# Attention in two blocks: heads paired by query block, weight rounding on ScalarE, and the sink as a column

## What is computed

```python
# block one, each of two layers
o_a = mla_attention(...)       # all 512 keys; q.k over 96 features, v of 64
o_c = windowed_gqa(...)        # keys of the blocks b-1, b, b+1; ALiBi bias; 64 features
m = max(max(s), sink); e = exp(s - m)
probs = e / (sum(e) + exp(sink - m))
# block two
yc = dsa_attention(...)        # causal, keys of the blocks 0..b, mask of the top 128; 64 features
```

## Time and profile before

| | |
|---|---|
| median of 3 runs | 2979.09 us (2977.27 to 2981.9) |
| the profiled execution, its own time | 2981.74 us |
| its span in the profile | 2979.9 us |
| TensorE busy | 2826.6 us, 95% |
| VectorE, ScalarE, GpSimd busy | 1519.9, 1077.5, 446.4 us |
| mean granted TensorE clock | 0.975 |

### The profile page before, as it was taken

How to read it: one execution, slowest core, us unless ns; L and a number is a source line. 1 busy time by engine, 2 the same in 40 slices (tenths; PEclk the granted TensorE clock), 3 DMA queues, 4 the chain that set the end, 5 groups by cost and what they waited for, 6 DMA issues and landing times. The chain is left out here.

```text
span 2979.9 us, 36682 instructions
## 1 busy us (share of the span) xinstructions
PE 2826.6 (95%) x13172; PEld 2236.6 (75%) x13172; DVE 1519.9 (51%) x2343; ACT 1077.5 (36%) x1713; POOL 446.4 (15%) x319
## 2 busy tenths in 40 slices
PE   5999999999999899999999999989998899899998
PEld 4874678888887687467888888767686588688886
DVE  5556673533324656667353333455588635643423
ACT  4345333422224534533342222443623324532221
POOL 1010111311102201011121110220101112211101
PEclk9999999999999899999999999999997899999999
DMA  3320012222222232001222222212231122122232
GB/s 130 125 88 29 29 58 86 84 99 96 101 100 99 75 118 85 29 29 57 96 75 99 98 100 99 99 59 83 77 121 57 43 85 71 57 85 94 90 112 85
DMA packets 37056, 245.92 MB, mean 83 GB/s; under 512 B 4144, under 2 KB 5168, under 8 KB 7984
## 3 DMA queue, kind: packets, MB, share of 16 engines
q1 hardware_dynamic: 33600, 239.09, 22.8%
q10 hardware_dynamic: 3312, 4.93, 0.5%
HBM read 241.91 MB, written 2.10 MB: 82 GB/s over the span
## 5 line engine op out<-in xcount | busy, mean ns | idle before, releaser
L529 PE MATMUL bank<-h_hi,w_hi 128*128 128x512 f32 (+1 forms) x2280 | 884.7, 388 | 22.6 <-DVE w_lo L1466 10.6
L531 PE MATMUL bank<-h_hi,w_lo 128*128 128x512 f32 (+1 forms) x2280 | 866.0, 380 | 0.0
L530 PE MATMUL bank<-h_lo,w_hi 128*128 128x512 f32 (+1 forms) x2280 | 865.8, 380 | 0.0
L1466 DVE TENSOR_TENSOR w_lo<-raw,w_hi 128x2048 fp32r<-128x2048 f32 x223 | 515.2, 2311 | 532.1 <-ACT w_hi L1011 373.6
L529 PEld LDWEIGHTS bank<-h_hi,w_hi 128*128 128x128 f32 x2280 | 432.2, 190 | 118.5 <-issue 30.6
L531 PEld LDWEIGHTS bank<-h_hi,w_lo 128*128 128x128 f32 x2280 | 432.1, 189 | 81.1
L530 PEld LDWEIGHTS bank<-h_lo,w_hi 128*128 128x128 f32 x2280 | 432.4, 190 | 79.2 <-issue 3.6
L1011 ACT ACTIVATE w_hi<-raw 128x2048 fp32r<-128x2048 f32 x141 | 269.3, 1910 | 225.0 <-PE bank L531 218.4
L529 PE MATMUL bank<-a_hi,w_hi 128*128 128x512 f32 x528 | 205.7, 390 | 0.0
L531 PE MATMUL bank<-a_hi,w_lo 128*128 128x512 f32 x528 | 205.7, 390 | 0.0
L530 PE MATMUL bank<-a_lo,w_hi 128*128 128x512 f32 x528 | 205.7, 390 | 0.0
(11 more groups left out here) (383 smaller groups left out, 4166.9 us busy)
## 6 DMA issues: line engine op xcount, KB each, us to landing
raw<-in_stream SPq DMA_DIRECT2D x226, 1024.0 KB, 4.9
x<-in_xT SPq DMA_DIRECT2D x2, 1024.0 KB, 12.6
out_T<-x ACTq DMA_DIRECT2D x8, 256.0 KB, 2.1
p_f<-in_pT ACTq DMA_DIRECT2D x2, 512.0 KB, 3.9
memf<-in_memT ACTq DMA_DIRECT2D x1, 1024.0 KB, 5.5
cst_sb<-in_cst ACTq DMA_DIRECT2D x1, 411.5 KB, 6.6
pos_i<-in_pos ACTq DMA_DIRECT2D x1, 258.0 KB, 9.2
vec<-in_vec ACTq DMA_DIRECT2D x2, 26.0 KB, 1.7
```

The source lines that it names most:

```text
L529: nc.tensor.matmul(ps, wh, xh, start=start, stop=False)
L530: nc.tensor.matmul(ps, wh, xl, start=False, stop=False)
L531: return nc.tensor.matmul(ps, wl, xh, start=False, stop=stop)
L1466: nc.vector.tensor_tensor(w_lo[s][:, :], raw[s][:, :], w_hi[s][:, :].bitcast(F32), ALU.subtract).then_inc(lo_ready, 1)
```

## The change

Three parts. **Order:** in `mla`, `gqa` and `dsa` the items go two heads at a time by query block: (0,b0), (1,b0), (0,b1), (1,b1) and so on (`items_of`). The value products move from once a head to once a query block of the pair (`values_of_pair`), and alternate between the two halves of the output. In the biased attentions both scores of a pair are issued together, at even steps, behind a wait until VectorE is through with the maximum of all items before (`shift_ready`). The output tile is taken at the next pair's first block. **Rounding:** ScalarE rounds the woven-in units (`split_unit` in ScalarE's `after_blocks`); GpSimd's `split_units` is gone. **Sink:** column 0 of each `gqa` probability tile holds sink/scale, which ScalarE writes; the maximum and the exponential run over it too. Two VectorE instructions an item go (L1661 or L1662, and L1671), and on ScalarE a one-column copy takes the place of the one-column exponential. The diff, cut:

```diff
-    stage("z1b", A=1, HP=1), stage("mla", I=32, H=8, O=4), stage("gqa", I=32, H=8, O=4),
-    stage("am", A=8, HP=1), stage("cm", A=8, R=8),
+    stage("z1b", A=1), stage("mla", I=32, H=16, O=4), stage("gqa", I=32, H=16, O=4),
+    stage("am", A=8), stage("cm", A=8, R=8),
...
+        def items_of(a):
+
+            if a["per_tile"] == 2:
+                return [(2 * pair + one, b) for pair in range(a["heads"] // 2) for b in range(ST) for one in range(2)]
+            return [(h, b) for h in range(a["heads"]) for b in range(ST)]
...
             def attention(c, st, ready, also=None):
                 a = ATT[st]
-                items = [(h, b) for h in range(a["heads"]) for b in range(ST)]
+                items = items_of(a)
                 for sem_, value in ready:
                     pe.wait_ge(sem_, value)
+                def scores(t):
+                    h, b = items[t]
+                    ks = a["keys"](b)
+                    nc.tensor.matmul(SCORES[t % 2][:, 0:len(ks) * P], a["q"](h, b), a["k"](h, ks),
+                                     start=True, stop=True).then_inc(logits_done, 1)
                 for t in range(len(items) + LAG):
-                    if t < len(items):
-                        h, b = items[t]
+                    if t < len(items) and a["biased"]:
+                        if t % 2 == 0:
+                            if t >= 2:
+                                pe.wait_ge(shift_ready, c.at("I", st, t))
+                            scores(t)
+                            scores(t + 1)
+                    elif t < len(items):
                         if t >= 2:
                             pe.wait_ge(exp_done, c.at("I", st, t - 1))
-                        ks = a["keys"](b)
-                        nc.tensor.matmul(SCORES[t % 2][:, 0:len(ks) * P], a["q"](h, b), a["k"](h, ks),
-                                         start=True, stop=True).then_inc(logits_done, 1)
+                        scores(t)
...
                             mm = nc.tensor.transpose(TURNED[:, j * P:(j + 1) * P],
-                                                     a["prob"][i % 4][:, j * P:(j + 1) * P], ident)
+                                                     a["prob"][i % 4][:, lo + j * P:lo + (j + 1) * P], ident)
                         mm.then_inc(turned, 1)
-                        if b == ST - 1 and h >= 1:
+                        if a["per_tile"] == 2:
+                            if i >= 2 and i % 2 == 0:
+                                values_of_pair(c, st, i // 2 - 1)
+                        elif b == ST - 1 and h >= 1:
                             values(c, st, h - 1)
                     if also is not None:
                         also(t)
-                values(c, st, a["heads"] - 1)
+                if a["per_tile"] == 2:
+                    values_of_pair(c, st, len(items) // 2 - 1)
+                else:
+                    values(c, st, a["heads"] - 1)
...
+            def values_of_pair(c, st, q):
+
+                a = ATT[st]
+                pair, b = q // ST, q % ST
+                pe.wait_ge(turn_taken, c.at("I", st, 2 * q + 2))
+                if b == 0 and (pair >= 1 or st != "mla"):
+                    pe.wait_ge(o_split, c.at("O", st, pair))
+                ks, at = a["keys"](b), slice(b * P, b * P + P)
+                for j, t in enumerate(ks):
+                    for one in range(2):
+                        mm = nc.tensor.matmul(VALUES[64 * one:64 * one + 64, at], a["v"](2 * pair + one, t), a["pT"][one][:, j, at],
+                                              start=j == 0, stop=j == len(ks) - 1)
+                mm.then_inc(head_done, 1)
...
-                items = [(h, b) for h in range(a["heads"]) for b in range(ST)]
+                items = items_of(a)
+
+                def set_sink(t):
+                    nc.scalar.activation(a["prob"][t % 4][:, 0:1], vv("sink", items[t][0]), ACT.Copy,
+                                         scale=1 / a["scale"]).then_inc(sink_set, 1)
+                for t in range(4) if sink else ():
+                    set_sink(t)
...
-                        if sink:
-                            nc.scalar.activation(st_snk[:, t:t + 1], vv("sink", h), ACT.Exp, bias=st_neg[:, t:t + 1])
+                        n += a.get("first", 0)
                         src = a["prob"][t % 4] if a["biased"] else SCORES[t % 2]
                         nc.scalar.activation(a["prob"][t % 4][:, 0:n], src[:, 0:n], ACT.Exp, bias=st_neg[:, t:t + 1],
                                              scale=a["scale"], accum_out=st_sum[:, t:t + 1]).then_inc(exp_done, 1)
+                        if sink and t + 4 < len(items):
+                            act.wait_ge(exp_done, c.at("I", st, t + 1))
+                            set_sink(t + 4)
                     if t >= LAG:
                         h, b = items[t - LAG]
-                        if b == ST - 1 and h >= 1 and h % a["per_tile"] == 0:
-                            output_hi(c, st, h // a["per_tile"] - 1)
+                        if a["per_tile"] == 2 and b == 0 and h % 2 == 0 and h >= 2:
+                            output_hi(c, st, h // 2 - 1)
+                        elif a["per_tile"] == 1 and b == ST - 1 and h >= 1:
+                            output_hi(c, st, h - 1)
...
+                    if b % BLK == BLK - 1 or b == TILES[st][-1][-1]:
+                        split_unit(c, st, b // BLK)
...
+                if t in (23, 31):
+                    split_unit(c, "mv", (t - 23) // 8)
...
-                            link(nc.vector.scalar_tensor_tensor(out=src[:, 0:n], in0=tile, scalar=factor, in1=SCORES[t % 2][:, 0:n],
+                            lo = a.get("first", 0)
+                            link(nc.vector.scalar_tensor_tensor(out=src[:, lo:lo + n], in0=tile, scalar=factor, in1=SCORES[t % 2][:, 0:n],
                                                                 op0=ALU.mult, op1=ALU.add))
+                            n += lo
+                        if sink:
+                            dve.wait_ge(sink_set, c.layer * len(items) + (t + 1))
                         link(nc.vector.reduce_max(st_max[:, t:t + 1], src[:, 0:n], AX_X))
-                        if sink:
-
-                            link(nc.vector.tensor_scalar(st_neg[:, t:t + 1], st_max[:, t:t + 1], a["scale"], vv("sink", h), ALU.mult, ALU.max))
-                            nc.vector.tensor_scalar(st_neg[:, t:t + 1], st_neg[:, t:t + 1], -1.0, None, ALU.mult).then_inc(shift_ready, 1)
-                        else:
-                            nc.vector.tensor_scalar(st_neg[:, t:t + 1], st_max[:, t:t + 1], -a["scale"], None, ALU.mult).then_inc(shift_ready, 1)
+                        nc.vector.tensor_scalar(st_neg[:, t:t + 1], st_max[:, t:t + 1], -a["scale"], None, ALU.mult).then_inc(shift_ready, 1)
+                    if a["per_tile"] == 2 and t % 8 == 3 and 11 <= t < len(items):
+                        output_lo(c, st, taken)
+                        taken += 1
                     if 1 <= t <= len(items):
...
-                        if sink:
-                            link(nc.vector.tensor_tensor(st_sum[:, i:i + 1], st_sum[:, i:i + 1], st_snk[:, i:i + 1], ALU.add))
                         link(nc.vector.reciprocal(st_rec[:, i:i + 1], st_sum[:, i:i + 1]))
-                        p = a["prob"][i % 4]
+                        p = a["prob"][i % 4][:, a.get("first", 0):]
                         nc.vector.tensor_scalar(p[:, 0:n], p[:, 0:n], st_rec[:, i:i + 1], None, ALU.mult).then_inc(prob_ready, 1)
...
-            def split_units(c, st):
-
-                for u, (kind, n) in enumerate(releases(st)):
-                    v = c.base[st]["U"] + u + 2
-                    pool.wait_ge(tile_done if kind == "T" else part_done, c.at(kind, st, n))
-                    pool.wait_ge(raw_ready[v % 2], c.raw(v))
-                    nc.gpsimd.tensor_tensor(w_hi[v % 2][:, :], raw[v % 2][:, :], ones[:, 0:1].to_broadcast([P, UC]), ALU.mult).then_inc(pool_hi_ready, 1)
```

64 lines of the change are left out of this document (19 added, 45 removed).

## The result

| | before | changed |
|---|---|---|
| median | 2980.49 us (2977.27 to 2982.55, 4 runs) | 2896.3 us (2893.83 to 2896.46, 4 runs) |
| span of the profiled execution | 2979.9 us | 2894.6 us |
| mean granted clock | 0.975 | 0.982 |

The account below looks back on a forecast made before the run. TensorE was taken as the bound; 2 x 15.2 (`gqa`) + 2 x (8.3 - 1.9) (`mla`) + 15 (`dsa`) = 58.2 us off 2981.7 gives 2923.5, by the runs' median 2921, stated as 2920; range 2893 to 2950 at 80%.

Parts of the forecast that it names:

- The frame: Whole kernel: TensorE is busy for 2826.6 of 2979.9 us, so its own work or its waits are what count.
- the forecast itself: Whole kernel: the main case, 2920 us, with its own range of 2900 to 2945 and a chance of 70%.
- rival 5: More than forecast: `dsa` returns to full clock early and no pair waits, 85 us gained, 2894 or a little less; 7%.
- Scores in pairs: In `gqa` and `dsa`, the second score of a pair is free: 11.7 us saved per `gqa`, 11.7 in `dsa` at full clock.
- Value products: Neighbours on different output halves overlap fully: 6.7 us saved per `gqa`, 8.3 per `mla`, 6.7 in `dsa` at full clock.
- Rival 1: Value products don't overlap at 128 columns: 55 us of the gain go, 2975, at best 2965; 8%.
- my ground for the overlap: At the end of `mla` before the change, 8 value records start within 1.30 us, so each half keeps its rate.
- `gqa`'s waits: In each `gqa`, TensorE waits for VectorE at the pairs of steps 12 and 28: 2 x 1.6 = 3.2 us lost.
- The rounding in `mla`: In each `mla`, a rounding on ScalarE falls where a step of TensorE is short: 1.9 us added on the path.
- 27 + 7 - 19: In `dsa`: 27 us of saved work at its mean clock, 7 of waits gone, 19 taken back: net 15, between 0 and 32.
- I take back 6 + 13 = 19: In `dsa`, waits for VectorE: four `w_lo` of some 1.5 us each, and 0.8 us at the other pairs.
- The signs: Changed profile: `gqa` at full clock, idle at most 10 us; scalings never 3 us; roundings 1.9 us, no wait for the copy.

Follow-up runs that it names:

- experiment 1: The kernel before with only the rounding of the woven-in weights moved from GpSimd to ScalarE, old order kept: 2967.8 us median, ratio 0.9972.
- experiment 2: The changed kernel with the rounding of the woven-in weights back on GpSimd: 2900.2 us median.
- experiment 1 to 5: Step from experiment 1 to the changed kernel with each `gqa` and `dsa` score issued at its own step again: 2923.2 us median.
- experiment 3: The changed kernel with the sink as before, a one-column exponential on ScalarE and two more VectorE instructions per `gqa` item: 2906.2 us median.

## Why the prediction was right or wrong

**The frame held.** TensorE's own time was what counted: its work at full clock fell by 73.9 us where I had 71.8. The time lies in the range, at its low end, but it is outside the 2900 to 2945 that I gave to the forecast itself with 70%. The likeliest was 24 us too high, and the range holds the result because it was stretched to take in most of rival 5, to which I gave 7%. Rival 5 had the size right and half of the reason: the clock of `dsa` came back, but it also said that no pair waits, and in `dsa` ten did.

**Scores in pairs: right.** Four records last as long as two (0.85 us), 11.7 us a `gqa`.

**Value products: right in mechanism, the size a little low in `mla`.** A group of `mla` takes 1.02 to 1.03 us and a step of 0.10 into it (four transposes take 0.53 before a group, 251.51 to 252.04, and 0.43 before a score); I had 1.19 with the step. What I missed is that the old groups paid that step too. By the trace an `mla` has 10.4 us less work, forecast 8.3. In `gqa` 8 groups at 0.59, 8 at 0.81 and a step of some 0.12 into each make 13.1 us (forecast 13.8). Rival 1 falls: its group would have lasted 2.1 us. One count in my ground for the overlap was off: the earlier trace rows counts records in flight, and 7, not 8, start within the 1.30 us; that each half keeps its rate stands.

**`gqa`'s waits: right.** 2.9 us at two places, forecast 3.2 at two. What I left out is that half of the woven-in blocks now lead into transposes, 0.08 us cheaper each: 1.3. 11.7 + 7.4 + 1.3 - 2.9 = 17.5, measured 17.1.

**The rounding in `mla`: wrong sign.** I had 1.9 us more of waits. In the old order it would have been nearly so: a wait of 1.7 us for the copy, and with the clock that fell behind it 3.0 (experiment 1). In the new one that wait is 0.7 us (the row at 260.23), since a value group of 1.02 us stands ahead of it, and the stage is 0.7 faster than with GpSimd's rounding (experiment 2). Idle time fell by 1.1 us in all: 3.0 to the good of the forecast. 6.4 + 2.1 (work) + 3.0 (waits) = 11.5, as measured.

**`dsa`: the two terms that failed.** The range was right; what was mis-sized is the sum of this paragraph, 27 + 7 - 19. Its 27 keeps the stage's clock at its old mean: 18.4 of work and 8.6 of clock. Its "I take back 6 + 13 = 19" are the waits, and the 13 counts 0.8 for all 16 pairs where the sentence leaves four out (12 would be 9.6). Measured from first to last score, 101.8 us became 76.7: 15.8 of work, 17.7 of half-clock loss as the mean clock rose from 0.75 to 0.90, and 8.4 more idle time, against the 12 that 19 less 7 gives. The waits for the scaled maximum are 13.3 us and those for probabilities 1.3. So here the clock gave 9 us more than forecast and the waits took 4 less, while the work fell short by 2.6.

The chain of experiments has the 25.0 us in steps. The rounding alone gives 13.2, all of it clock. Items in pairs with their value products (experiment 1 to 5) give 6.8: 5.2 of work and 3.7 of idle time, with 2.2 given back to the clock. Scores in pairs give 5.0: 11.6 of work and 6.5 of clock against 13.1 of idle time. The steps depend on their order: in the new order the rounding is worth 4.5 in `dsa` (experiment 2).

**The signs.** `gqa` had full clock and 2.9 us idle, and roundings on ScalarE take 1.9 us. Scalings on VectorE are at most 0.49. One sign failed: in `mla` TensorE does wait for the copy behind a rounding, 0.7 us.

**What stays open**: why the half clock lasts 38 us at the start of `dsa` in one order and a few in another. The runs show that it depends on VectorE's work there and not on the wait ahead alone; they do not give a rule. Nor do they say why parts with the same code differ in clock from run to run, by 5 us behind `dsa` (experiment 3).

## What to carry to other kernels

A stage that runs in part at half clock should be forecast with its clock as a case of its own, one at the old mean and one at full: here the clock moved by as much (17.7 us) as the work that the edit removed (15.8). When matmuls of a pair are issued together, look for the last *reader* of their banks and wait for that, not for the next semaphore that happens to be there: it was worth 10 us of 2896, and putting those readers first another 5. In this kernel two heads on two halves of the array's rows or columns came at the price of one, and four records of one half in a row hardly spoiled it (0.06 us a group).

## What the runs showed of the hardware

- Products that contract over the same 128 rows and write different 64-column halves overlap: 16 records in 1.02 us, with 0.43 for the step from 8 to 16 (0.59 to 1.02), 0.054 a record. In the trace the records start two by two, 0.006 us apart, and each half's next one 0.109 us later, as with one half alone. This is the stretch of one group of the changed kernel, records of L705 alone:

```profile
252.03:253.06 1.03, 1.02 (x16) 0.85 (x16) 1.00 0.96 398
```

  The Trainium skill (TensorE: Matmul & The Clock Gate, "The mechanism") has a load overlap running matmuls only when its row group differs. The measurement decides: here the rows are the same, and in 1.03 us a load is in flight for 0.85 and a matmul for 1.02. The Trainium skill (TensorE: Matmul & The Clock Gate, "LDWEIGHTS (loading the stationary operand)") gives an estimate of 53 ns for a load of 64 columns, by which the loads of a group would take 0.85 us. The trace doesn't show them set the pace: each half keeps the 0.109 us that it has alone.
- TensorE looks past queued records of one half to start the other: with eight of one half ahead, four started alone; with four ahead, the other half started within 0.013 us, and a group of 16 in runs of four lost 0.06 us (1.08 against 1.02).
- A product of two float32 constants, 128x512, took 0.87 us at full clock (11 in 9.6 us), where one of the kernel's three rounded products takes 0.23.
- VectorE's scaling of a probability tile took at most 0.49 us in the kernels in which ScalarE rounds the woven-in weights. In the kernel before, ten took 2.2 to 3.8 us, each beside a rounding on GpSimd.
- A whole stage can lose more TensorE busy time (80.1 to 61.9 us) than it gains in length (81.7 to 76.7), and still be granted more clock (0.82 to 0.90).
